# Dilated attention by residue classes with a merge stage, and a new place for the first coarse piece of the sparse attention

## The reference, cut to what matters

```python
DIL_GROUPS = ((128, 1), (512, 4), (2048, 16))     # window, dilation; 4 heads each, SEQ = 512

def dilated_attention(q, k, v, bias_table):
    outs = []
    for g, (w, d) in enumerate(DIL_GROUPS):
        sl = slice(g * A_HEADS_PER_GROUP, (g + 1) * A_HEADS_PER_GROUP)
        outs.append(dilated_window_group(q[:, :, sl], k[:, :, sl], v[:, :, sl], w, d, bias_table[:, sl]))
    m_all = jnp.stack([m for _, m, _ in outs])
    scale = jnp.exp(m_all - jnp.max(m_all, axis=0))
    num = sum(scale[g][..., None] * outs[g][0] for g in range(len(DIL_GROUPS)))
    den = sum(scale[g] * outs[g][2] for g in range(len(DIL_GROUPS)))
    return num / den[..., None]
```

## Time and profile before

| | us |
|---|---|
| three runs | 2806.19, 2808.58, 2806.55 |
| their median | 2806.55 |
| the profiled execution's own time | 2794.94 |
| its span, first to last instruction | 2793.1 |
| mean granted clock of TensorE in it | 0.927 |

### The profile page before, as it was taken

How to read it: one execution, slowest core, us unless ns; L and a number is a source line. 1 busy time by engine, 2 the same in 40 slices (tenths; PEclk the granted TensorE clock), 3 DMA queues, 4 the chain that set the end, 5 groups by cost and what they waited for, 6 DMA issues and landing times. The chain is left out here.

```text
span 2793.1 us, 31379 instructions
## 1 busy us (share of the span) xinstructions
PE 2493.5 (89%) x11301; PEld 1888.2 (68%) x11301; DVE 1054.2 (38%) x2017; ACT 952.2 (34%) x1432; POOL 352.3 (13%) x367
## 2 busy tenths in 40 slices
PE   4898686998699989799999899977997998899999
PEld 2586574656388868478878578933554886588877
DVE  4744534333444532332222322174435333322222
ACT  1332112333345532244421222274345432344311
POOL 0001321121012210011100000023223000111100
PEclk6998897879799999899999999986898999999999
DMA  7751001002133332133332233101001332233331
GB/s 260 255 169 31 1 1 43 23 1 61 30 98 98 96 92 83 30 90 98 98 98 83 60 83 98 50 4 46 1 31 46 91 103 61 72 94 97 109 93 61
DMA packets 347879, 212.19 MB, mean 76 GB/s; under 512 B 20252, under 2 KB 327122, under 8 KB 347757
## 3 DMA queue, kind: packets, MB, share of 16 engines
q1 hardware_dynamic: 342848, 202.64, 24.6%
q10 hardware_dynamic: 4942, 8.43, 0.8%
HBM read 208.35 MB, written 9.24 MB: 78 GB/s over the span
## 5 line engine op out<-in xcount | busy, mean ns | idle before, releaser
L225 PE MATMUL ffn_up_psum<-ffn_h_hi,ffn_up_w_hi 128*128 128x512 f32 x704 | 275.5, 391 | 0.0
L226 PE MATMUL ffn_up_psum<-ffn_h_lo,ffn_up_w_hi 128*128 128x512 f32 x704 | 274.1, 389 | 0.0
L227 PE MATMUL ffn_up_psum<-ffn_h_hi,ffn_up_w_lo 128*128 128x512 f32 x704 | 274.0, 389 | 0.0
L307 DVE TENSOR_TENSOR ffn_up_w_lo<-ffn_up_raw,ffn_up_w_hi 128x1024 fp32r<-128x1024 f32 x88 | 107.7, 1225 | 338.6 <-ACT ffn_up_w_hi L303 338.6
L303 ACT ACTIVATE ffn_up_w_hi<-ffn_up_raw 128x1024 fp32r<-128x1024 f32 x88 | 93.3, 1062 | 196.8 <-PE ffn_up_psum L227 193.8
L225 PEld LDWEIGHTS ffn_up_psum<-ffn_h_hi,ffn_up_w_hi 128*128 128x128 f32 x704 | 132.5, 188 | 28.7 <-DVE ffn_up_w_lo L307 1.3
L226 PEld LDWEIGHTS ffn_up_psum<-ffn_h_lo,ffn_up_w_hi 128*128 128x128 f32 x704 | 132.3, 188 | 28.2 <-issue 0.8
L227 PEld LDWEIGHTS ffn_up_psum<-ffn_h_hi,ffn_up_w_lo 128*128 128x128 f32 x704 | 132.3, 188 | 27.6
L225 PE MATMUL conv_up_psum<-h_hi,conv_up_w_hi 128*128 128x512 f32 x352 | 137.4, 390 | 0.0
L225 PE MATMUL ffn_down_psum<-ffn_hidden_hi,ffn_down_w_hi 128*128 128x512 f32 x352 | 137.3, 390 | 0.0
L226 PE MATMUL ffn_down_psum<-ffn_hidden_lo,ffn_down_w_hi 128*128 128x512 f32 x352 | 136.9, 389 | 0.0
(11 more groups left out here) (614 smaller groups left out, 5587.9 us busy)
## 6 DMA issues: line engine op xcount, KB each, us to landing
conv_up_raw<-in_ffn_up_dram SPq DMA_DIRECT2D x44, 512.0 KB, 3.7
ffn_up_raw<-in_ffn_w_gate_dram SPq DMA_DIRECT2D x44, 512.0 KB, 3.7
ffn_up_raw<-in_ffn_w_up_dram SPq DMA_DIRECT2D x44, 512.0 KB, 3.7
ffn_down_raw<-in_ffn_w_down_dram SPq DMA_DIRECT2D x32, 704.0 KB, 4.5
in_a_mod_slots<-in_ada_w_dram SPq DMA_DIRECT2D x16, 1024.0 KB, 7.1
branches_raw<-in_w_in_dram SPq DMA_DIRECT2D x24, 512.0 KB, 3.6
down_raw<-in_ffn_down_dram SPq DMA_DIRECT2D x16, 704.0 KB, 4.3
mod_slots<-in_ada_w_dram SPq DMA_DIRECT2D x4, 2048.0 KB, 15.3
```

Of the source, the lines that this page charges most:

```text
L225: pe.matmul(out, w_hi, r_hi, start=start, stop=False)
L226: pe.matmul(out, w_hi, r_lo, start=False, stop=False)
L227: return pe.matmul(out, w_lo, r_hi, start=False, stop=stop)
L307: dve.tensor_tensor(self.lo[:, j % PAIRS], self.raw[:, j], self.hi[:, j % PAIRS].bitcast(F32), ALU.subtract)\
```

## The change

**Residue classes.** The groups 1 and 2 of the dilated attention are computed by residue class: class r holds the tokens r, r + 4, r + 8, ... (`RESIDUES` = 4, 128 tokens each). Within a class group 1 sees all earlier tokens, and group 2 every fourth. A *wide* piece (`SidePiece`) is one slot and one class: 128 queries against 128 keys of group 1 and beside them 128 keys of group 2, 256 columns in all, scored by two matmuls whose queries and keys are read with a stride of four numbers. A *near* piece is group 0 as before, but a unit of its own. There are 16 near and 16 wide units, all of one piece, in four groups: near units of slots 0 and 1, their wide units, then the same for slots 2 and 3. Query tiles now go up from 0 to 3. The minima and sums of all units are kept (`stats`) and each group is normalised by itself.

**Merge.** A new stage joins near and wide outputs: the logarithm of the sums less the minima, laid along the partitions of the output by 32 small matmuls with a broadcast column as weights and the identity as moving operand, the difference's sigmoid, and near times share plus wide.

**Values.** The values of groups 1 and 2 are computed as column jobs into `o` (free at that time) and turned by TensorE, class by class, with 16 transposes at the ends of the two `vb` jobs.

**Fillers.** In the dilated attention's first 9 pieces TensorE runs one extra matmul of 128x256 ahead of each score, into the bank that the score then overwrites.

**Sparse attention.** The first coarse piece is inserted behind two 512-key units. As units now may be weighed that early, TensorE waits for the copied coarse piece before it opens an output.

**Tables.** The dilated attention loads four tables of 128x256 and eight of 128x128 in place of twelve of 128x512.

```diff
-    near, far = bucket(128), bucket(2048)
-    kinds = [(near, dist >= 0), (far, (dist >= 0) & (dist <= 128)), (far, (dist >= 0) & (dist % 4 == 0)),
-             (far, (dist >= 0) & (dist % 16 == 0)), (far, dist >= 0)]
+    near, far, apart = bucket(128), bucket(2048), bucket(2048, RESIDUES)
+    kinds = [(near, dist >= 0), (far, (dist >= 0) & (dist <= 128)), (apart, dist >= 0),
+             (apart, (dist >= 0) & (dist % RESIDUES == 0)), (far, dist >= 0)]
...
+                if tokens == "turned":
+                    source, columns = c
+                    pe.wait_ge(stored, kept[source])
+                    for r in range(RESIDUES):
+                        mm = pe.transpose(psum[:, i % 4, r * P:(r + 1) * P], columns[:, r::RESIDUES], attention.ident)
+                    mm.then_inc(done, 1)
+                    continue
...
+class SidePiece:
...
+    def score(self, pe, psum):
+        for n, (q, k, _) in enumerate(self.heads):
+            mm = pe.matmul(psum[:, n * P:(n + 1) * P], q, k, start=True, stop=True)
+        return mm
...
+def filler_columns(score):
+    keys = 0 if score is None or score.coarse else score.keys
+    lacking = 0.85 * max(600 + 0.95 * keys, 750 + 0.8 * keys) - max(60, 2 * keys / 2.4)
+    return min(int(lacking * 2.4 / 4) // 32 * 32, T // 2)
...
+                    if cover_fill and i < weigh_lag + 2:
+                        filler = filler_columns(x)
+                        pe.matmul(psum[:, i % 4, 0:filler], attention.ident,
+                                  flat(attention.square[:, 0:TT])[:, 0:filler], start=True, stop=True)
+                    x.score(pe, psum[:, i % 4, 0:x.keys]).then_inc(scored, 1)
...
                     if unit.coarse is not None and c == 0:
                         piece, h = unit.coarse
+                        opened = [n for n, p in enumerate(pieces) if p[2] is piece][0]
+                        pe.wait_ge(copied[opened % 2], opened // 2 + 1)
                         piece.open(pe, out, h, unit.tile)
...
         units.insert(COARSE_AT, Unit([coarse[1]], 0, None, None))
-        units.insert(0, Unit([coarse[0]], 0, None, None))
+        units.insert(COARSE_FIRST, Unit([coarse[0]], 0, None, None))
...
+                    for i in range(TT):
+                        lo = max(0, i - 1)
+                        units.append(Unit([Piece(
+                            qa[rows, slot // 2, i * P:(i + 1) * P], qa[rows, (A_HEADS + slot) // 2],
+                            lambda j, slot=slot: va[:, j, slot * HD:(slot + 1) * HD], lo, (i + 1 - lo) * P,
+                            near_tables[:, slot, 0 if i else P:], table_no=3 * slot)], 2 * pair, rows, i))
...
+                            heads.append((qa[rows, head // 2, r::RESIDUES], qa[rows, (A_HEADS + head) // 2, r::RESIDUES],
+                                          va[:, r, head * HD:(head + 1) * HD]))
...
+                      stats=(least, sums), cover_fill=True)
+        merge_by_denominators(nc, old, least, sums, near, wide, out)
...
+            act.activation(every, sums[:, :, 0], ACT.Ln).then_inc(logged, 1)
+            for pair in range(2):
+                act.wait_ge(laid, pair + 1)
+                act.activation(along[:, pair, 0], psum[:, 2 * pair], ACT.Copy).then_inc(kept, 1)
+                act.wait_ge(subtracted, pair + 1)
+                act.activation(share[:, pair], along[:, pair, 1], ACT.Sigmoid).then_inc(shared, 1)
...
+            pe.wait_ge(lowered, 1)
+            for pair in range(2):
+                for kind in range(2):
+                    for i in range(TT):
+                        at = slice(i * P, (i + 1) * P) if kind == 0 else slice(i, T, RESIDUES)
+                        for a in range(2):
+                            mm = pe.matmul(psum[a * HD:(a + 1) * HD, 2 * pair + kind, at],
+                                           logs[:, pair, kind, a, i:i + 1].to_broadcast([P, HD]),
+                                           attention.ident, start=True, stop=True)
+                mm.then_inc(laid, 1)
...
+            dve.wait_ge(logged, 1)
+            dve.tensor_tensor(every, every, least[:, :, 0], ALU.subtract).then_inc(lowered, 1)
+            for pair in range(2):
+                c.add(dve.tensor_tensor(by_rank(near[:, pair]), by_rank(near[:, pair]), near_order[pair], ALU.subtract))
...
+            for pair in range(2):
+                dve.wait_ge(shared, pair + 1)
+                c.link(dve.tensor_tensor(near[:, pair], near[:, pair], share[:, pair], ALU.mult))
+                dve.tensor_tensor(by_rank(out[:, pair]), by_rank(near[:, pair]), near_order[pair], ALU.add)
...
-            jobs = [tok_job(VA + c * 256, 256, lambda i, c=c: va[:, i, c * 256:(c + 1) * 256]) for c in range(3)]
-            jobs += [tok_job(VB + c * 256, 256, lambda i, c=c: vb[:, i, c * 256:(c + 1) * 256]) for c in range(2)]
+            va_wide = o[:, 0:4]
+            jobs = [cols_job(VA + c * 256, 2, lambda n, c=c: va_wide[:, 2 * (c - 1) + n]) for c in range(1, A_GROUPS)]
+            jobs += [tok_job(VA, 256, lambda i: va[:, i, 0:256])]
+            for c in range(2):
+                loads, width, outputs = tok_job(VB + c * 256, 256, lambda i, c=c: vb[:, i, c * 256:(c + 1) * 256])
+                outputs += [("turned", c, n, va_wide[:, 2 * c + n], va[:, :, (2 + 2 * c + n) * P:(3 + 2 * c + n) * P])
+                            for n in range(2)]
+                jobs.append((loads, width, outputs))
```

More of the change, by code:

```diff
@@ L421, in mixed_products @@
                     outs.append((n, o[1], None, [(0, T, o[2], o[3])]))
+                elif o[0] == "turned":
+                    _, job, nth, columns, dst = o
+                    source = [i for i, other in enumerate(outs) if other[0] == job][nth]
+                    outs.append((n, (source, columns), "turned", [(0, T, dst, ACT.Copy)]))
                 else:
@@ L1483, in attention @@
         turned = s.sb("turned", [P, TURNED, T])
-        peak = s.sb("peak", [P, 8, 4])
-        sums = s.sb("sums", [P, 8, 4])
-        weight = s.sb("weight", [P, 8])
+        ring = 8 if stats is None else n_units
+        peak, sums = [s.sb(n, [P, ring, 4]) for n in ("peak", "sums")] if stats is None else stats
+        weight = s.sb("weight", [P, ring])
         spacer = s.sb("spacer", [1, 8])
@@ L1520, in _ @@
                     continue
[L1521 removed]
+                pool.tensor_scalar(b, b, weight[:, u % ring:u % ring + 1], units[u].factor, ALU.mult, ALU.mult)\
                     .then_inc(scaled, 1)
@@ L1535, in _ @@
                         pe.wait_ge(biased, i - 3)
-                    cols = slice(x.lo * P, x.lo * P + x.keys)
-                    if x.coarse:
-                        mm = x.score(pe, psum[:, i % 4, 0:x.keys])
-                    else:
-                        mm = pe.matmul(psum[:, i % 4, 0:x.keys], x.q, x.k[:, cols], start=True,
-                                       stop=x.extra is None)
-                    if x.extra is not None:
-                        mm = pe.matmul(psum[:, i % 4, 0:x.keys], x.extra[0], x.extra[1][:, cols],
-                                       start=False, stop=True)
-                    mm.then_inc(scored, 1)
+                    if cover_fill and i < weigh_lag + 2:
[3 more added lines that the diff above has]
+                    x.score(pe, psum[:, i % 4, 0:x.keys]).then_inc(scored, 1)
                 t = i - turn_lag
@@ L1615, in _ @@
                     u, c, x = pieces[i]
-                    for n in x.tables_read if x.coarse else [x.table_no]:
+                    for n in x.tables_read:
                         dve.wait_ge(tabled[n], 16)
@@ L2151, in dilated_attention @@
 def dilated_attention(nc, old, qa, va, tables_dram, out):
-    with nc.sbuf_tensor("dil_tables", [P, A_HEADS, T], F32) as tables:
-        units = []
-        for slot in range(A_SLOTS):
-            rows = slice(slot % 2 * HD, (slot % 2 + 1) * HD)
-            for i in reversed(range(TT)):
-                pieces = []
-                for g in range(A_GROUPS):
-                    head = g * A_SLOTS + slot
-                    lo = max(0, i - 1) if g == 0 else 0
-                    pieces.append(Piece(
-                        qa[rows, head // 2, i * P:(i + 1) * P], qa[rows, (A_HEADS + head) // 2],
-                        lambda j, head=head: va[:, j, head * HD:(head + 1) * HD],
-                        lo, (i + 1 - lo) * P, tables[:, head, (TT - 1 - i + lo) * P:], table_no=slot * A_GROUPS + g))
-                units.append(Unit(pieces, slot // 2, rows, i))
-        order = [g * A_SLOTS + slot for slot in range(A_SLOTS) for g in range(A_GROUPS)]
-        attention(nc, old, "dil", units, [(tables[:, head], tables_dram[TAB_A + head]) for head in order],
-                  lambda act, g, o: act.activation(out[:, g], o, ACT.Copy))
+    near_keys, units_of = 2 * P, 2 * 2 * TT
@@ new lines, in dilated_attention, with sb @@
+    with ExitStack() as ctx:
+        def sb(name, shape):
```

(31 more changed lines are left out.)

78 lines of the change are left out of this document (59 added, 19 removed).

## The result

The changed kernel takes 2772.4 us (median; 2769.6 to 2774.2), the kernel before, run beside it, 2807.6 us (2806.2 to 2828.3): ratio 0.986, 95% interval 0.981 to 0.990. The forecast was 2782 with a range of 2760 to 2812, so the change is faster, as said, and 10 us faster than said. The profiled execution has 2771.48 us and a span of 2769.7, 23.4 less than the span before; the sum in the prediction had -24.8. Nearly the same number came out for other reasons, which the profile shows at once.

The account below looks back on a forecast made before the run. TensorE's work and clock were taken as the bound. Terms of -50.5 + 22.0 + 2.6 + 1.1 + 0 = -24.8 us took the profiled 2794.94 to 2770.1, and 11.6 carried over gave 2781.8, range 2760 to 2812.

Parts of the forecast that it names:

- the sum in the prediction: Whole kernel: dilated attention, merge, selected attention's cold start, projections and sparse attention together change the time by -24.8 us.
- It supposes that the clock, once up, stays: Dilated attention: the 2.01 us idle gap in the fill should go, so all 59.3 us are priced at the high clock.
- rival (d): Strided wide scores +9.4, merge's strided results +7.8, clock falling among wide units +19.6: slower, 2818.6 us; chance 0.14.
- the three signs: Wrong if sparse attention has no low stretch, dilated attention has a 0.50 stretch, or wide scores take 0.63 or 1.6 us.
- The dil stage: Dilated attention: 32 one-piece units, fillers and drain take 59.3 us in place of 109.8, saving 50.5 us.
- rival (c): Dilated attention: the fillers don't help and the clock falls in the fill as before: +19.6 us, 2801; chance 0.10.
- The merge: New stage after the dilated attention, with nothing beside it: adds 22.0 us, 15.7 of them matmuls.
- I price its 32 matmuls (64 columns of broadcast weights, 128 moving) at the low clock by the weighing matmuls: Merge stage: 0.49 us each, 15.7 us in all; at the high clock 8 us less.
- The projections: Projection stage: two jobs turned into column jobs -1.6 us, 16 added transposes +2.7: net +1.1 us (+0.2 to +2.9).
- Nsa: Sparse attention: moving the first coarse piece behind two wide units keeps the clock's fall; booked at 0 us.
- Rival (b): Sparse attention keeps its high clock because two wide units stand ahead: 2762 us; chance 0.12.
- I carry the difference over: Whole kernel: the runs' median lies 11.6 us above the profiled execution, added to 2770.1 to give 2781.8 us.

Follow-up runs that it names:

- kernel 3: Changed kernel with queries and keys of the wide scores read from adjoining columns (wide part on the wrong tokens): 2744.1 us.
- kernel 12: Changed kernel, strides kept, with a 256-column filler ahead of every wide score, 16 more: 2761.3 us.
- kernel 6: Changed kernel with the wide heads laid out by residue class in the normalising stage and without the nine fillers: 2737.6 us, ratio to before 0.976.
- kernel 1: Changed kernel with the sparse attention's first coarse piece ahead of the two wide units again: 2770.8 us.
- kernel 4: Kernel before with only the sparse attention's first coarse piece moved behind two wide units, and the wait for its copy: 2805.4 us, ratio to before 0.9995.
- kernel 5: Changed kernel with the wide heads laid out by residue class in the normalising stage, fillers kept: 2745.8 us.

## Why the prediction was right, and where not

**The clock in dil.** The failed step is "It supposes that the clock, once up, stays". It named the fill's gap as what had brought it down, and a shorter fill as the cure. The fill was shorter, and the clock fell in the wide units: 21 us, 1.5 of them in the merge (kernels 3 and 12). Of rival (d), given a chance of 0.14, this is the part on the clock; its strided scores came to +2.9 us of +9.4, and its strided results to nothing of +7.8. The 61.5 us at 0.50 in dil are one of the three signs that I had named as proving the forecast's reasons wrong.

**The dil stage.** First score to last weighing took 1988.73 - 1906.3 = 82.4 us, not 59.3: it saved 27.4, not 50.5. Of the 23.1 us between, the wide score has 16 x (1.23 - 1.05) = 2.9 (within its bounds), the fillers 9 x (0.63 - 0.47) = 1.4, and the rest, 18.8, is the clock's, less a little that other terms had too much. In kernel 3 the same span takes 53.4 us (1909.98 to 1963.38), 29.0 less; without the 9.4 of the strides 19.6 remain for the clock. The rest of the sum was sound: without fillers and strides it would have been 59.3 - 4.2 - 16 x (1.05 - 0.64) = 48.5 us, and kernel 6 has 47.4. The rule on 16-byte lines of the Trainium skill's page "SBUF — State Buffer", which would have put the wide score near its upper bound of 1.64 us, was right in direction; the trace has 1.23.

**The fillers** were rival (c)'s subject. They indeed don't help; but what they failed to prevent was in the wide units, not in the fill, and they cost 4.1 to 4.9 us of the stage.

**The merge** came to 13.6 - 0.94 = 12.7 us, not 22.0. The step that failed is "I price its 32 matmuls (64 columns of broadcast weights, 128 moving) at the low clock by the weighing matmuls": the clock was low for only 3.06 of the 5.24 us, and in kernel 3, after the same 2.70 us of idle time, not at all. The price itself was the larger error: 0.12 us at the high clock in kernel 3 where weighing has 0.29. By that row the lower bound, too, was misread: 32 x 0.29 = 9.3 is 6.4 us less than 15.7, not 8. The tail is 5.69 us where 3.4 and the 0.94 make 4.3. That the selected attention starts cold was right: +2.9 for +2.6.

**The projections** cost +2.7 us for +1.1, inside their bounds, but most of it is the clock's. From the first matmul of the jobs that the change touches to the first behind them, all at the high clock, kernel 1 (with the change's jobs) and the kernel before have

```profile
1695.95:1754.26 58.31, 58.31 (x400) 1.00 0.31 87
1709.87:1767.57 57.70, 57.70 (x481) 1.00 0.31 88
```

The jobs' own price is thus +0.6 us. One term was too dear, the transposes: 16 x 0.11 = 1.8 us, its lower bound, for 2.7. The other 2.1 us go with the clock, for which the sum had nothing here: the changed kernel's profile has 6.75 us at 0.50 near the stage's start (1694.25 to 1701.0), where the kernel before has none.

**Nsa** was booked at 0, and kernels 1 and 4 confirm that. Rival (b), by which nsa keeps its clock, looks half true in the profile (12 of 19.5 us) and is not: the low stretch is there in every profile, and it is as short without the move (kernel 1).

**From the profile to the median** a second step failed: "I carry the difference over". The 11.6 us by which the median lay over the profiled execution go with a lower clock: of 17 runs of the kernel before, the five under 2800 us had a mean granted clock of 0.923 to 0.926, the ten from 2807 to 2815 had 0.917 to 0.921, and the two above had 0.913. The changed kernel's profiled execution lies within 1 us of its median. So against the median of before the change gains 35 us, 12 more than between the profiles. Kernel 4's 88.5 us stretch shows one way in which this can happen; that the typical run of before has it, or has it in dil, is not shown.

Together, against the sum of -24.8: dil +23.1, merge -9.3, projections +1.6, selected attention +0.3, nsa -12.0 (luck), all else -2.3 (with the dilated attention's warm-up) make +1.4, hence the -23.4 between the spans. Errors of 25 us one way and 24 the other cancelled, which is luck, and the 10.7 us too much that were carried over (11.6 where the changed kernel has 0.9) made the total too high.

## What to carry to other kernels

Where TensorE is the bound, ask of every new operand not only what its stride costs, but how much TensorE still streams beside it: here a stride that cost 9 us took the clock with it and cost 30. Move a rearrangement to an engine with time to spare in the stage ahead (GpSimd wrote with the stride at 0.01 us apiece; the stage grew by 2.5 us, where kernels 5 and 6 gained 27 and 35), and only then see whether fillers earn anything. And before a difference between two profiles is explained, look at the spread of the runs: a stretch at the low clock had 17 or 48 us in the same stage of kernels whose programs are the same there.

## What was not expected of the hardware

- A 128-key fp32 score with a stride of four numbers on both operands takes 0.61 us at either clock, where adjoining columns take 0.32 at the high one. One strided operand of the two costs three quarters or more of the extra time (1.08 and 1.13 us for two scores against 1.22). Transposes with every-fourth weights take 0.11 us each all the same.
- Strided results in PSUM cost TensorE nothing here (32 matmuls in 5.38 us either way), and strided reads and writes in SBUF cost GpSimd 0.01 us of 1.25.
- TensorE can be busy for all of 61.5 us and have the low clock all the time; in the same stage, with 10 us more of dense matmuls or with adjoining operands, it has the high clock throughout.
- A broadcast column of weights against the identity takes 0.12 us for 128 columns in fp32 at the high clock (0.16 to 0.19 where the clock was low for part of it), less than half of the 0.29 of a weighing matmul of this shape.
